# A two-layer S5 / HGRN2 decoder step on one core: HGRN's sample values spread by transfers, a narrower first level, one table product and one memory column moved

## The chip, the cores and the metric

One core of a Trainium2 chip runs the whole kernel; nothing is shared with other cores. The metric is the device time of one launch in microseconds (us), taken as the median of several runs. TensorE is called PE in the profile, VectorE DVE, ScalarE ACT, GpSimd POOL and SyncE SP.

## The reference, cut to what matters

Two layers process 512 prompt tokens and 8 sample rows, each of width 1024. A layer is a half-step SwiGLU FFN, a mixer, cross-attention into 256 memory tokens, and a second half-step FFN. The mixer of layer 0 is S5, that of layer 1 is HGRN2 with 8 heads, each with a 128 x 128 state.

```python
def trunk(x, s5_re, s5_im, hg_s, mem_k, mem_v, lower_bounds, p):
    for i in range(DEPTH):
        x = x + 0.5 * swiglu(rmsnorm(x, ...), p['ffn1_w_in'][i], p['ffn1_w_out'][i])
        h = rmsnorm(x, p['mix_norm'][i])
        if i % N_MIXERS == 0: y, hr, hi = s5_mixer(h, ...)
        else:                 y, sn = hgrn2_mixer(h, hg_s[j], ...)
        x = x + y
        x = x + cross_attend(rmsnorm(x, ...), mem_k[i], mem_v[i], ...)
        x = x + 0.5 * swiglu(...)
# HGRN2, one chunk of 64 tokens of one head:
        att = jnp.einsum('bthk,bshk,btshk->bhts', qc, kc, decay)
        s_new = jnp.exp(btot)[..., None] * s + jnp.einsum('bshk,bshv->bhkv', k_dec, vc)
# for a sample row (one token): S = diag(f) S + k v^T, o = S^T q
# S5: bu from b_bar = (lam_bar - 1) / lam * b, a complex scan over time, y = Re(C h) + d u
# memory: kk, vv = split(rmsnorm(mem, g) @ w_kv)
```

## The kernel before

**Tiles.** Activations are held feature-major, as columns of 520 tokens (512 prompt, 8 sample), split into a front of 256 and a rear of 264. Weights stream from HBM by SP in pieces of 128 output columns ("chunks"). ACT rounds a chunk to w_hi (line 1330), DVE computes the remainder w_lo (line 1827), and PE makes three products for each tile: hi x hi and lo x hi in line 3019, hi x lo in line 3024. A chunk with 1024 input rows is 48 matmuls. The work of the mixers is put between such chunks, on the same in-order PE queue. Small products go to the four PSUM banks called mis, large ones to those called lin.

**The order of small products.** Lists written in the kernel (PREP and K_OUT, S5_ORDER and KV_AFTER, HG; lines 613 to 685) give groups of small products in order. Each group fills one bank, bank number = group number modulo 4, and `reuse` makes PE wait until the group four places earlier was emptied by DVE or ACT. Which chunk a group follows is fixed by the hooks of the lists.

**S5's tables.** While layer 0's first FFN runs, POOL computes for each pair of groups a the tables sFe and sGe (lines 1179 to 1191; each is three operations of lines 736 to 738). PE transposes sFe (groups F, line 2560) and multiplies sGe with bZ (group K, lines 2567 and 2570). Each pair a = 0..3 has its F, F, K behind chunk pair a of the output projection, which has 11 row blocks (66 matmuls a chunk). POOL alternates between two buffers of sGe; for table a it waits for K(a-2).

**Memory columns.** In S5's mixer itself, PE transposes and folds the inputs (X, U, FU, Y groups; line 2732 is U and FU) while ACT and DVE scan. Sixteen column blocks of the memory's keys and values (kv 0 to kv 15, line 2512, three times 8 products each) are spread over it. kv 0, 1 and 2 follow FU 15, the last of the fold groups. The first needs m_hi and m_lo, the normalized memory tokens, which SP reloads from HBM with two transfers of 1 MB (line 818).

**HGRN.** hg_in runs 8 iterations of four chunks (plus two to drain). Between the chunks of head h stand the small products of head h-1 and h-2: S (the sample's output row from the state sS, line 2786), V and K (transposes of values and keys, line 2800), A (attention by level: level 32, 16, 8 in line 2812 from decayed copies lvl, and the diagonal in line 2815), T and N, D (state increments, line 2838), **B** (line 2820: the value column of each of the 8 sample rows, broadcast to 128 columns and transposed, so that a bank holds it on every partition; two groups of four), O (outputs, lines 2853 and 2861) and R (line 2876). DVE updates the prompt state in `states` (lines 2202, 2206) and then the sample states with eight operations (line 2316), sS = value x key + sS, which read B's banks. Then it splits the next weights. SP's queue in an iteration: weights (line 966), prompt state out (908), sample states out (910), the next head's sample states in (921).

## Time and profile before

| | us |
|---|---|
| median of 3 runs (2360.42 to 2362.08) | 2360.5 |
| the profiled execution, whole | 2360.95 |
| its span in the trace | 2359.2 |
| PE busy in the span | 2335.6 (99%) |
| DVE / ACT / POOL busy | 1295.1 / 869.1 / 605.4 |
| mean granted TensorE clock | 0.998 |

PE is busy for all but 24 us of the span. So an edit matters only by what it takes from PE's queue, by the waits of PE that it makes or ends, and by the stretches in which PE is granted less than its full clock; in the clock column 1.00 is 2.4 GHz and 0.50 is 1.2 GHz. A timeline row groups neighbouring instructions of one kind: where it starts, how long it lasts, how many (x), and in brackets how long the engine sat idle before it and what released it. Some products are recorded as two instructions.

### The profile page before, as it was taken

To read this page: it belongs to the slowest core of one execution; us is meant where nothing else is said; L and a number is where in the kernel's file an instruction comes from. 1 tells how busy PE (TensorE), PEld (TensorE's weight loads), DVE (VectorE), ACT (ScalarE), POOL (GpSimd) and SP (SyncE) were. 2 spreads that over 40 slices of the span, in tenths; PEclk is the share of its full clock that TensorE was granted. 3 is DMA by queue.
4 is the path that set the end of the run, shared out by engine and by line. 5 is a ranking of instruction groups with operands and counts; after the bars stand their busy time and mean duration, and the time that the engine had idled before them with its cause. 6 is when DMAs were issued, how large, how long until landed. Compare 5 with 4: busy or idle time off the path is not lost.

```text
span 2359.2 us, 50146 instructions
## 1 busy us (share of the span) xinstructions
PE 2335.6 (99%) x21043; PEld 2273.7 (96%) x21043; DVE 1295.1 (55%) x1906; ACT 869.1 (37%) x1399; POOL 605.4 (26%) x591
## 2 busy tenths in 40 slices
PE   9999999999999999999999999999999999999999
PEld 8999999889979999999999999999999979999999
DVE  6653643964576443445543344577777666443443
ACT  4432333453233321322433233267775233321323
POOL 3779967431103000004111010432122102000003
PEclk9999999999999999999999999999999999999999
DMA  5456445553563333333543333233332653333332
GB/s 160 130 160 153 122 136 165 175 171 107 161 245 86 98 99 89 98 96 98 159 118 111 100 108 115 83 100 107 104 108 77 214 188 91 97 94 94 98 94 94
DMA packets 483707, 289.19 MB, mean 123 GB/s; under 512 B 22289, under 2 KB 466962, under 8 KB 482514
## 3 DMA queue, kind: packets, MB, share of 16 engines
q1 hardware_dynamic: 477856, 280.66, 40.3%
q0 software_dynamic: 560, 1.84, 0.6%
q10 hardware_dynamic: 5122, 4.25, 0.5%
q8 instruction: 129, 2.11, 0.4%
q14 instruction: 40, 0.33, 0.0%
HBM read 258.86 MB, written 27.85 MB: 122 GB/s over the span
## 4 chain that ended last, share of the span: by engine, by line
PE 91%; DVE 4%; POOL 2%; ACT 1%; issue 1%; DMA 1%; SPq 0%; DVEq 0%; POOLq 0%; ACTq 0%
PE lin L3019 51%; PE lin L3024 25%; PE mis L2512 4%; PE mis L2650 1%; PE mis L2633 1%; POOL sTmp L737 1%; PE lin L2600 1%; PE lin L2762 1%; PE lin L2981 1%; PE lin L2757 1%; POOL sGe L738 0%; PE lin L2650 0%; DVE w_lo L1827 0%; PE mis L2626 0%; POOL sFe L738 0%
## 5 line engine op out<-in xcount | busy, mean ns | idle before, releaser
L1827 DVE TENSOR_TENSOR w_lo<-raw,w_hi 128x1024 fp32r<-128x1024 f32 (+1 forms) x322 | 463.8, 1440 | 294.4 <-ACT w_hi L1330 293.7
L1330 ACT ACTIVATE w_hi<-raw 128x1024 fp32r<-128x1024 f32 (+1 forms) x328 | 365.1, 1113 | 311.3 <-PE lin L3024 257.7
L3019 PE MATMUL lin<-a_rear,w_hi 128*128 128x264 f32 x3552 | 455.6, 279 | 0.0
L3019 PE MATMUL lin<-a_front,w_hi 128*128 128x256 f32 x3552 | 451.6, 279 | 1.1 <-DVE a_rear L1840 0.7
L3019 PEld LDWEIGHTS lin<-a_rear,w_hi 128*128 128x128 f32 x3552 | 432.7, 188 | 0.0
L3019 PEld LDWEIGHTS lin<-a_front,w_hi 128*128 128x128 f32 x3552 | 424.5, 188 | 4.6 <-issue 1.8
L3024 PE MATMUL lin<-a_rear,w_lo 128*128 128x264 f32 x1776 | 245.1, 278 | 0.0
L3024 PE MATMUL lin<-a_front,w_lo 128*128 128x256 f32 x1776 | 240.6, 277 | 0.9 <-DVE w_lo L1827 0.9
L2391 DVE SCALAR_TENSOR_TENSOR xT<-lin,xT 128x520 f32<-128x520 f32 (+1 forms) x87 | 60.8, 699 | 322.9 <-PE lin L3024 322.2
L1063 POOL TENSOR_TENSOR acc<-xT 128x520 f32<-128x520 f32 x8 | 12.2, 1520 | 864.0 <-DVE xT L2391 836.0
L3024 PEld LDWEIGHTS lin<-a_rear,w_lo 128*128 128x128 f32 x1776 | 223.8, 188 | 0.0
L3024 PEld LDWEIGHTS lin<-a_front,w_lo 128*128 128x128 f32 x1776 | 219.6, 188 | 1.6 <-DVE w_lo L1827 1.5
L1741 ACT ACTIVATE f_front<-t 128x256 fp32r<-128x256 f32 (+1 forms) x88 | 36.9, 419 | 398.3 <-DVE t L2372 398.3
L3019 PE MATMUL lin<-f_rear,w_hi 128*128 128x264 f32 x1386 | 179.9, 283 | 0.0
L3019 PEld LDWEIGHTS lin<-f_rear,w_hi 128*128 128x128 f32 x1386 | 172.1, 189 | 0.2
L3019 PE MATMUL lin<-f_front,w_hi 128*128 128x256 f32 x1386 | 170.3, 276 | 0.0
L3019 PEld LDWEIGHTS lin<-f_front,w_hi 128*128 128x128 f32 x1386 | 163.3, 188 | 0.0
L1737 ACT ACTIVATE t<-t 128x520 f32<-128x520 f32 x88 | 56.5, 642 | 270.4 <-DVE t L2366 270.4
L2370 DVE TENSOR_TENSOR t<-lin,rstd 128x520 f32<-128x520 f32 x88 | 61.5, 699 | 161.4 <-PE lin L3024 161.4
L1067 POOL TENSOR_TENSOR sqt<-xT 128x520 f32 (+1 forms) x54 | 81.9, 1517 | 211.0 <-DVE xT L2391 148.8
L3019 PE MATMUL lin<-g_all,w_hi 128*128 128x264 f32 (+1 forms) x1024 | 128.8, 278 | 0.0
L3019 PEld LDWEIGHTS lin<-g_all,w_hi 128*128 128x128 f32 x1024 | 122.7, 188 | 1.1 <-DVE g_all L1967 1.1
(512 smaller groups left out, 3182.7 us busy)
## 6 DMA issues: line engine op xcount, KB each, us to landing
raw<-in_ffn_w_in_dram SPq DMA_DIRECT2D x176, 512.0 KB, 3.9
raw<-in_ffn_w_out_dram SPq DMA_DIRECT2D x64, 704.0 KB, 4.6
kc<-in_cache_mem_k_dram SPq DMA_DIRECT2D x32, 512.0 KB, 6.8
vc<-in_cache_mem_v_dram SPq DMA_DIRECT2D x16, 1024.0 KB, 9.7
raw<-in_hg_w_in_dram SPq DMA_DIRECT2D x32, 512.0 KB, 4.2
raw<-in_xattn_w_kv_dram SPq DMA_DIRECT2D x16, 512.0 KB, 4.4
raw<-in_s_w_glu_dram SPq DMA_DIRECT2D x16, 512.0 KB, 3.9
raw<-in_xattn_w_q_dram SPq DMA_DIRECT2D x16, 512.0 KB, 3.9
```

The costliest lines, as they stand in the source:

```text
L737: link(eng.tensor_tensor(tmp, pv[1], mv[1 - e], ALU.mult))
L1067: step.link(pool.tensor_tensor(sqt[:], tile(xT, m), tile(xT, m), ALU.mult))
L1330: act.activation(w_hi[:, j, 0:kt, :], raw[:, j, 0:kt, :], ACT.Copy).then_inc(hi_ready, 1)
L1737: act.activation(t2[:], t1[:], ACT.Silu).then_inc(gate_out, 1)
L1741: ins = act.activation(tile(out, i), t3[:, cols], ACT.Copy)
L1827: dve.tensor_tensor(low_weights(n, j), raw[:, j, 0:kt, :], w_hi[:, j, 0:kt, :].bitcast(F32), ALU.subtract).then_inc(lo_ready, 1)
L2370: step.link(dve.tensor_tensor(t4[:], lflat(1), rstd[:], ALU.mult))
L2391: dve.scalar_tensor_tensor(out=tile(xT, m), in0=lflat(j), scalar=scale, in1=tile(xT, m), op0=ALU.mult, op1=ALU.add)\
L2512: ins = pe.matmul(kv_bank(c)[:, 0:NM], w[:, e, k, :], x[:, k, :], start=k == 0 and u == 0, stop=k == KD - 1 and u == 2)
L2600: ins = pe.matmul(lin[32 * h:32 * h + NS, 1, 0, 0:NM], pZ[:, t, h, b, :], vc[layer][V_SLOT[b]][:, t, h * NM:(h + 1) * NM], start=False, st ...
L3019: pe.matmul(lpart(j, half), high[:, k, :], (x_lo if u else x_hi)[half][:, k, :], start=start and u == 0 and k == 0, stop=False)
L3024: ins = pe.matmul(lpart(j, half), low[:, k, :], x_hi[half][:, k, :], start=False, stop=k == kt - 1)
```

## The change

There are four edits.

1. **Sample values by transfer.** PE's B groups are gone. For each head SP writes the 128 x 8 sample values from hgV to a scratch in HBM (`values_out`, elements of 4 bytes), and later reads them back into vB with a source that repeats the 8 rows of 128 values for each of the 128 partitions (`values_spread`, 512 KB in runs of 512 bytes). DVE's eight sample operations read vB in place of a PSUM bank and count in a new semaphore, `sampled`, on which PE's S group, ACT's next hgF and SP's hg_s transfer wait. For head 0 the sample operations stand behind the split of the next weights; the last head's two transfers stand behind the second load of hg_out's weights. A head has 15 groups instead of 17, so the groups four places earlier change: the O groups wait for N and A's diagonal group, no longer for D; the R groups wait for D.
2. **First level.** The level with 32 tokens (HC is 64) multiplies with the 32 early columns as weights, not with all 64.
3. **Table product.** K(2) moves from behind pair 2 of the output projection to the start of what follows pair 3, ahead of F 6, F 7 and K(3).
4. **Memory column.** kv 0 moves from behind FU 15 to behind FU 11.

```diff
+    vB = [at(f"vB{e}", [P, NS, P], F32, (o_hid + 6 * HTILE, o_tmp + 5 * TILE)[e]) for e in range(2)]
+    hg_v = nc.dram_tensor("hg_v", (HH, NS, P), F32, kind="Internal").ap()
...
         if 0 <= g < HH:
-            made += [("D", (g, 0), "dve"), ("D", (g, 1), "dve"), ("B", (g, 0), "dve"), ("B", (g, 1), "dve")]
+            made += [("D", (g, 0), "dve"), ("D", (g, 1), "dve")]
             made += [("O", (g, 0), "act"), ("O", (g, 1), "act")]
...
+    (late, end), (_, after_late) = PREP["ffn1_out0", 0, 2], PREP["ffn1_out0", 0, 3]
+    PREP["ffn1_out0", 0, 2], PREP["ffn1_out0", 0, 3] = (late, end - 1), (end - 1, after_late)
...
+        if (what, a) == ("FU", 11):
+            S5_ORDER += [("kv", c) for c in KV_AFTER[None][:1]]
         if q + 1 == S5G.after("FU"):
-            S5_ORDER += [("kv", c) for c in KV_AFTER[None]]
+            S5_ORDER += [("kv", c) for c in KV_AFTER[None][1:]]
...
+            def values_out(h):
+                sp.wait_ge(used[0], first_pair["hg_in", 1] + 2 * h + 2)
+                sp.dma_start(hg_v[h].rearrange("b v -> v b"), hgV[h % 2][:, SEQ:NT],
+                             allow_slow_non_contiguous=True).then_inc(spread_out, 16)
+            def values_spread(h):
+                sp.wait_ge(spread_out, 16 * (h + 1))
+                if h >= 2:
+                    sp.wait_ge(sampled, h - 1)
+                    sp.wait_ge(spread_in, 16 * h)
+                src = bass.AP(tensor=hg_v.tensor, offset=h * NS * P, ap=[[0, P], [P, NS], [1, P]])
+                sp.dma_start(vB[h % 2][:], src).then_inc(spread_in, 16)
...
                         if first and j == 1 and ST[n][0] == "hg_out":
+                            values_out(HH - 1)
+                            values_spread(HH - 1)
                             for h in range(HH - 2, HH):
                                 states(h)
...
                             sample_states_in(i // 2)
-                        elif i >= 4:
-                            states(i // 2 - 2)
+                            if i >= 3:
+                                values_spread(i // 2 - 1)
+                        elif i >= 2:
+                            values_out(i // 2 - 1)
+                            if i >= 4:
+                                states(i // 2 - 2)
...
                 def values(p, b):
                     dve.wait_ge(chunk_done, 2 * p + 3)
+                    if p >= p0 + 4:
+                        dve.wait_ge(spread_out, 16 * ((p - p0) // 2 - 1))
...
+                def sample_states(g):
+                    dve.wait_ge(spread_in, 16 * (g + 1))
+                    for f in range(2):
+                        dve.wait_ge(hg["s_decay"], 2 * g + f + 1)
+                        for u in range(4):
+                            s_ = 4 * f + u
+                            ins = dve.scalar_tensor_tensor(
+                                out=sS[g % 2][:, s_], in0=vB[g % 2][:, s_],
...
-                    if 0 <= g < HH:
-                        for f in range(2):
-                            q = G.at("B", (g, f))
...
+                    if 0 < g < HH:
+                        sample_states(g)
                     if 0 < h < HH:
                         split(p + 2, 0, hg_chunk(h, 2))
+                    if g == 0:
+                        sample_states(g)
...
                 if what == "S":
-                    G.emptied_of(pe, "B", (a, 1))
+                    pe.wait_ge(sampled, a + 1)
...
-                            ins = pe.matmul(bank[rows, t * HC // 2:(t + 1) * HC // 2].rearrange("p (b t) -> p b t", t=level),
-                                            lvl[u][:, c], late, start=True, stop=True)
+                            early = level if 2 * level == HC else HC
+                            ins = pe.matmul(bank[rows.start:rows.start + early, t * HC // 2:(t + 1) * HC // 2]
+                                            .rearrange("p (b t) -> p b t", t=level),
+                                            lvl[u][:, c.start:c.start + early], late, start=True, stop=True)
```

PE's queue around the table products of pairs 2 and 3 (L2560 is F, L2567 and L2570 are K; f_front and f_rear are the FFN's hidden activations), first in the kernel before, behind the second chunk of pair 2:

```order
L3024 MATMUL lin<-f_rear_61,w_lo_1_58 128x264 x11
L2560 MATMUL mis<-ident,sTF_235 128x128 x8
L2567 MATMUL mis<-sGe_199,bZ 32x128 x8
L2570 MATMUL mis<-dD,ident 32x16 x4
L3019 MATMUL lin<-f_rear_61,w_hi 128x264 x11
```

and after, at the same place and behind pair 3:

```order
L3054 MATMUL lin<-f_rear_61,w_lo_1_58 128x264 x11
L2595 MATMUL mis<-ident,sTF_237 128x128 x8
L3049 MATMUL lin<-f_rear_61,w_hi 128x264 x11
...
L3054 MATMUL lin<-f_rear_61,w_lo_1_58 128x264 x11
L2602 MATMUL mis<-sGe_201,bZ 32x128 x8
L2605 MATMUL mis<-dD,ident 32x16 x4
L2595 MATMUL mis<-ident,sTF_237 128x128 x8
L2602 MATMUL mis<-sGe_202,bZ 32x128 x8
```

K(2) has passed two chunks and now stands directly ahead of F 6, F 7 and K(3).

PE's queue in S5's mixer at the end of the fold groups (L2732, after the change L2767) and the start of the memory columns (L2512, after the change L2547), before:

```order
L2732 MATMUL lin<-sU,sTF_236 64x80 x24
L2732 MATMUL mis<-sU,sTF_236 64x80 x16
L2732 MATMUL lin<-sU,sTF_236 64x80 x24
L2512 MATMUL mis<-m_hi_103,w_hi 128x256 x8
L2512 MATMUL mis<-m_lo_105,w_hi 128x256 x8
```

and after:

```order
L2767 MATMUL lin<-sU,sTF_238 64x80 x24
L2767 MATMUL mis<-sU,sTF_238 64x80 x8
L2547 MATMUL mis<-m_hi_103,w_hi 128x256 x8
L2547 MATMUL mis<-m_lo_105,w_hi 128x256 x8
L2547 MATMUL mis<-m_hi_103,w_lo_56 128x256 x8
L2767 MATMUL mis<-sU,sTF_238 64x80 x8
L2767 MATMUL lin<-sU,sTF_238 64x80 x24
```

The three times 8 products of kv 0 now split the fold groups: 32 products stand behind them.

SP's queue in one iteration of hg_in, from the second weight pair to the next one, before:

```order
L908 DMA out_hg_p_dram<-hS 128x128 [waits hg_void_dve]
L910 DMA out_hg_s_dram<-sS_177 128x8x128 [waits hg_void_dve]
L966 DMA raw<-in_hg_w_in_dram 128x8x128 [waits lo_ready] x2
L921 DMA sS_177<-in_state_hgrn_dram 128x8x128 [waits hg_fill,hg_s_out]
L966 DMA raw<-in_hg_w_in_dram 128x8x128 [waits lo_ready] x2
```

and after:

```order
L923 DMA hg_v<-hgV_162 128x8x1 [waits used0]
L916 DMA out_hg_p_dram<-hS 128x128 [waits hg_void_dve]
L918 DMA out_hg_s_dram<-sS_177 128x8x128 [waits sampled]
L989 DMA raw<-in_hg_w_in_dram 128x8x128 [waits lo_ready] x2
L944 DMA sS_177<-in_state_hgrn_dram 128x8x128 [waits hg_fill,hg_s_out]
L933 DMA vB_187<-hg_v 128x1024 [waits spread_in,sampled,spread_out]
L989 DMA raw<-in_hg_w_in_dram 128x8x128 [waits lo_ready] x2
```

Two transfers joined the queue: one ahead of the states' outputs, one behind the load of the next sample states.

## Rows read from the trace of the kernel before

**Rows 1.** The page's part 1: busy us, share of span, instructions.

```profile
PE 2335.6 (99%) x21043; PEld 2273.7 (96%) x21043; DVE 1295.1 (55%) x1906; ACT 869.1 (37%) x1399; POOL 605.4 (26%) x591
```

**Rows 2.** Waits of PE: engine line, releaser: us in total, times, longest.

```profile
PE lin L2732 <- issue: 2.1, 1, 2.1
...
PE mis L2853 <- DVE hS L2206: 0.8, 1, 0.8
```

**Rows 3.** Timeline of PE, one head of HGRN (start, us, what).

```profile
1648.60 1.09 PE L2820 MATMUL mis<-ident,hgV 128*128 128x128 f32 x8
1649.45 2.13 PE L3019 MATMUL lin<-a_front,w_hi 128*128 128x256 f32 x16
...
1659.89 1.07 PE L3024 MATMUL lin<-a_front,w_lo 128*128 128x256 f32 x8
...
1665.29 1.59 PE L2812 MATMUL mis<-lvl 128*64 128x32 f32 x48
1666.81 0.44 PE L2792 MATMUL mis<-ident,sRow 128*128 128x128 f32 x2
```

**Rows 4.** Timelines of PE and DVE, head 0 of HGRN.

```profile
1595.67 1.19 PE L3024 MATMUL lin<-a_front,w_lo 128*128 128x256 f32 x8 [0.51 <-DVE w_lo L1827]
...
1591.49 2.15 DVE L2316 SCALAR_TENSOR_TENSOR sS<-mis,hgK,sS 128x128 f32<-128x128 f32 x8
1593.56 2.06 DVE L1827 TENSOR_TENSOR w_lo<-raw,w_hi 128x1024 fp32r<-128x1024 f32 x1
```

**Rows 5.** Timeline of DVE, the next iterations and the last head.

```profile
1650.29 0.69 DVE L2188 TENSOR_TENSOR hgV<-lin,rstd 128x520 f32<-128x520 f32 x1
...
1655.90 1.21 DVE L1827 TENSOR_TENSOR w_lo<-raw,w_hi 128x1024 fp32r<-128x1024 f32 x1
...
1685.88 2.16 DVE L2316 SCALAR_TENSOR_TENSOR sS<-mis,hgK,sS 128x128 f32<-128x128 f32 x8
...
1798.25 2.06 DVE L2316 SCALAR_TENSOR_TENSOR sS<-mis,hgK,sS 128x128 f32<-128x128 f32 x8
```

**Rows 6.** Timeline of SP, and the transfers issued in 1640:1700.

```profile
1664.44 0.37 SPq L921 DMA_DIRECT2D sS<-in_state_hgrn_dram  x1
...
sS<-in_state_hgrn_dram SPq DMA_DIRECT2D x2, 512.0 KB, 4.7
```

**Rows 7.** Timeline of PE at the table products of pairs 2 and 3.

```profile
196.92 0.64 PE L2567 MATMUL mis<-sGe,bZ 128*32 128x128 f32 x16 [2.84 <-POOLq L1191]
197.36 0.26 PE L2570 MATMUL mis<-dD,ident 128*32 128x16 f32 x8
197.54 4.47 PE L3019 MATMUL lin<-f_rear,w_hi 128*128 128x264 f32 x22
...
215.88 0.64 PE L2567 MATMUL mis<-sGe,bZ 128*32 128x128 f32 x16 [0.31 <-ACT sTF L1462]
```

**Rows 8.** Timeline of POOL at the same place.

```profile
193.87 2.86 POOL L738 TENSOR_TENSOR sGe<-sGe,sTmp 128x576 f32<-128x576 f32 x1
...
214.26 1.42 POOL L738 TENSOR_TENSOR sGe<-sGe,sTmp 128x576 f32<-128x576 f32 x1
```

**Rows 9.** Windows: us, busy PE, PEld, DVE, ACT, POOL; PEclk, DMA, GB/s.

```profile
197.30:216.30 19.00, 18.69 (x176) 18.45 (x168) 6.08 (x5) 3.69 (x5) 17.27 (x13) 0.91 0.50 116
```

**Rows 10.** Timelines of PE and DVE at the first memory columns.

```profile
434.69 1.61 PE L2732 MATMUL lin<-sU,sTF 128*64 128x80 f32 x41 [2.05 <-issue]
436.23 1.20 PE L2512 MATMUL mis<-m_hi,w_hi 128*128 128x256 f32 x8
...
438.97 0.29 DVE L2130 COPY sFH<-hs 128x128 f32<-128x128 f32 x1
```

**Rows 11.** Timeline of SP, and the transfers issued in 426:446.

```profile
427.05 0.43 SPq L818 DMA_DIRECT2D m_lo<-mem_split  x1
...
m_lo<-mem_split SPq DMA_DIRECT2D x1, 1024.0 KB, 8.0
```

**Rows 12.** Windows of 1 us, as in rows 9, at the stall.

```profile
433.00:434.00 1.00, 0.00 (x0) 0.00 (x0) 0.96 (x2) 0.00 (x0) 0.00 (x0) 1.00 0.35 131
```

More of the change, by code:

```diff
@@ L453, in trunk_kernel @@
            "scaled_dve", "front", "state_out", "s_decay", "s_out", "squares", "inverse")}
-    rows_in = [sem(f"rows_in{b}") for b in range(NS)]
+    rows_in = [sem(f"rows_in{b}") for b in range(4)]
+    spread_out, spread_in, sampled = sem("spread_out"), sem("spread_in"), sem("sampled")
     consts_done = sem("consts_done")
@@ L2308, in hg_in @@
                         states(g)
-                    if 0 <= g < HH:
-                        for f in range(2):
-                            q = G.at("B", (g, f))
-                            dve.wait_ge(hg["s_decay"], 2 * g + f + 1)
-                            dve.wait_ge(hg["fill"], q + 1)
-                            for u in range(4):
-                                s_ = 4 * f + u
-                                ins = dve.scalar_tensor_tensor(
-                                    out=sS[g % 2][:, s_], in0=hg_bank(q)[:, u * P:(u + 1) * P],
-                                    scalar=hgK[g % 2][:, SEQ + s_:SEQ + s_ + 1], in1=sS[g % 2][:, s_],
-                                    op0=ALU.mult, op1=ALU.add)
-                            ins.then_inc(hg["void_dve"], 1)
+                    if 0 < g < HH:
+                        sample_states(g)
                     if h == HH:
```

14 lines of the change are left out of this document (5 added, 9 removed).

## The prediction, made before the changed kernel was run

> **What bounds the kernel now.** I read the page's busy times first: PE is busy for 2335.6 us of a span of 2359.2 [rows 1]; no other engine comes near. So time can only be won from PE's own instructions, its waits, or stretches at a lower clock. The list of PE's waits comes next: of its entries behind the kernel's start the largest two are at places that the change touches, 2.84 us at the table product (released by POOL) [rows 7] and 2.1 us in the fold groups (released by nothing that the profile shows), and another touched one is 0.8 us at HGRN's outputs [rows 2]. Then I read the timelines of PE, DVE, SP and POOL there. I sum against the profiled execution, 2360.95 us; the median of the runs is 0.45 us lower, and I take that off at the end.
>
> **Edit 1, the sample values.** What leaves PE: the eight transposes start at 1648.60 and the next chunk starts at 1649.45, a slot of 0.85 us [rows 3]. They stand in every one of the 8 heads: 8 x 0.85 = 6.8 us. Nothing waits there for another engine, so the chunks behind move up by that much, if the others follow.
>
> Do they? DVE: the remainder w_lo is split from 1655.90 for 1.21 us, so it ends at 1657.11 [rows 5]; PE takes it at 1659.89 [rows 3], 2.78 us later. With PE 0.85 us earlier 1.9 us are left. The sample multiplies of DVE stay (8 in 2.15 us), with another source. SP: the values are written by DVE from 1650.29 for 0.69 us [rows 5], so they can be sent from 1651.0. The spread is issued behind the load at 1664.44 [rows 6], near 1664.9, and is needed by the multiplies of the next iteration at 1685.88 [rows 5]: 21 us. Its size is that of the load of sS, which landed after 4.7 us [rows 6]. The first transfer is 1024 elements of 4 bytes, which no row shows: from nothing to some 10 us, and 14 us lie between the two issues. I count both at nothing; the cover is the 21 us and the 14 us. On SP's queue the spread puts about 0.4 us (a transfer's issue, as the row at 1664.44) ahead of the next two loads of weights, which wait for DVE's splits and not for SP.
>
> Head 0 is tighter: there PE waits 0.78 us for DVE's states [rows 2], and 0.51 us for w_lo, which DVE makes from 1593.56, behind the multiplies of 2.15 us at 1591.49 [rows 4]. In the new order these multiplies stand behind that split, so the 0.51 us go. The 0.78 us: the O groups now reuse banks that A and N emptied, and only the second half of the outputs, which reads the states, needs them; the 16 products ahead of it cover the wait. So head 0 keeps its 0.85 and gains 0.5. In the last head S waits for the multiplies, which run from 1798.25 for 2.06 us [rows 5]; of that head's 0.85 about 0.25 is turned into a wait. Sum: -6.8 - 0.5 + 0.25 = -7.05 us, with bounds -7.3 (all of it) and -5.8 (head 0's whole and the last head's slot lost).
>
> The Trainium skill has a rule that speaks against this edit (SBUF — State Buffer, "Who interferes with whom"): a DVE instruction with two SBUF inputs contends with a GpSimd instruction that reads SBUF, and the one that starts first keeps the shared ports for its whole length; the multiplies now have two SBUF inputs instead of one. The trace agrees so far as POOL's line 738 takes 2.86 us at one time and 1.42 at another [rows 8]. By that rule the multiplies could be held up by one POOL instruction in each head, which the 1.9 us above would take up; the sum would not change.
>
> **Edit 2, the first level.** Line 2812's 24 products take 1.52 us, from 1665.29 to 1666.81 [rows 3]: 63 ns each. Products with 32 columns as weights are seen elsewhere: eight of line 2567 in 0.44 us (55 ns, 128 moving columns), four of line 2570 in 0.18 us (45 ns, 16 moving columns) [rows 7]. The changed eight have 32 moving columns; at 50 ns they save 8 x 13 = 0.1 us a head. But a tile of another size now stands in front of the second level. I take -0.1 a head, -0.8 in all, since the 1.52 us already hold one such change; bounds are -1.7 (all eight at 37 ns) and +0.8 (the extra change costs 0.2 and nothing is saved).
>
> Edits 1 and 2 together: **-7.9 us**, between -9.0 and -5.0.
>
> **Edit 3, the table product.** It should end the 2.84 us at 196.92 and the slow stretch behind it. Behind the wait PE runs at a lower clock: the window 197.3 to 216.3 has 0.91 of full clock, so 19.0 x 0.09 = 1.7 us are lost in it [rows 9], and its first 22 products take 4.47 us [rows 7]. Both look like a gain of 4.5 us. But behind the next two chunks stands K(3), at 215.88 [rows 7], and its table comes from POOL at 214.26 + 1.42 = 215.68 [rows 8]. POOL was busy for 17.27 of those 19.0 us [rows 9] and has no slack; its work isn't touched. So PE can't pass that place before 215.9, whatever it wins ahead of it. Without the wait and the slow stretch PE comes there 2.84 + 1.7 = 4.5 us earlier and waits 4.5 + 0.3 us there instead of 2.84 once. That is zero, and then the slow clock: before, it followed the wait and lay ahead of POOL's gate, where it cost nothing; now it follows the longer wait and lies behind the gate, where nothing takes it up: +1.7 us. It is paid only if the clock falls again; after 2.84 us of idle it did, so after 4.8 I expect it. DVE's splits also fall earlier relative to POOL's table, and one more POOL operation can be 1.4 us longer (2.86 against 1.42, [rows 8]); I put 0.3 on that. Edit 3: **+2.0**, bounds 0 (no fall of the clock) and +3.1 (1.7 + 1.4).
>
> **Edit 4, the memory column.** It moves work into the 2.05 us stall that ends at 434.69 [rows 10]. But kv 0 needs m_lo, issued at 427.05, which landed 8.0 us after: 435.05 [rows 11], later than the end of the stall. So the stall is not filled. When does PE reach kv 0 behind FU 11? The stall began at 434.69 - 2.05 = 432.64. Behind FU 11 stand 8 products in mis and 24 in lin, 64 records, of which 41 ran behind the stall, in 436.23 - 434.69 = 1.54 us or 0.038 each [rows 10]; the other 23 ran ahead of it in 0.9. So PE is there at 431.75 and waits to 435.05: 3.3 us in place of 2.05, which is +1.3, and the 64 records follow. If the stall itself came from something that is done by 434.7, it is not added. Two more changes of tile size are in the queue, some 0.1 us. DVE has finished its scan at 438.97 [rows 10]; the first output group comes behind kv 2, later at either time, so nothing else is late. The clock stayed at 1.00 in the stall of 2.05 us [rows 12]; it fell behind the one of 2.84. With 3.3 us I expect a fall, and take 1.4 us for it (somewhat under the 1.7 above, since more of what follows is light work). Edit 4: **+2.8**, bounds +0.4 (the transfers land 1 us earlier, no fall) and +3.3.
>
> **The sum.** -7.9 + 2.0 + 2.8 = -3.1 us, so 2357.85 against the profiled 2360.95, and 2357.4 as a median.
>
> **The rivals.**
> - *One gate or both, but no fall of the clock.* PE was at full clock through the 2.05 us stall, which speaks for it; the fall at 198 us speaks against it. Then edit 3 is +0.3, edit 4 is +1.4: -6.2, 2354.3 us.
> - *The moves do what they seem meant for.* Both waits vanish and the clock with them: -7.9 - 2.84 - 1.7 - 2.05 = -14.5, 2346.0 us. For it speaks that the rows of the waits stand just there; against it that POOL's table ends at 215.68 and m_lo lands at 435.05 whatever PE does. It would need POOL to be released by PE somewhere, which its rows don't show.
> - *The transfer is late (slower).* vB is read 128 times from one piece of 4 KB, which no row shows. The mechanism: DVE waits for it in front of the multiplies, and PE behind that for w_lo, in each of 8 heads. It decides when landing takes more than 21 + 1.9 = 23 us, against 4.7 for a plain load of the same size. At 24.5 us it costs 1.5 x 8 = +12: with the rest, 2369.4 us.
> - *The clock falls longer, or the drain between tile sizes costs all of edit 2's bound:* +1.6 and +1.1 on the sum, 2360.1 us, no change.
>
> The Trainium skill says of tile sizes (TensorEngine Tiling (Array Packing), "Key Properties") that changing the mode drains the engine. Edit 2 adds one such change a head and edit 4 two; by that rule edit 2 would lie at its upper bound and the total near 2359, which is within the range.
>
> **How the numbers follow.** My forecast with its bounds has a chance of 0.55, the rival without a fall of the clock 0.20, that with both waits gone 0.08, the late transfer 0.07, the last one 0.10. The predicted time is 2357.4. The range goes from 2352.5 (below the rival without a fall, with edits 1 and 2 at their best) to 2361.0 (above the last rival); outside lie the two rivals of 0.08 and 0.07 and a little of the rest. A measurement of this kernel can tell 0.2%, 4.7 us, from no change: below 2355.8 is faster, above 2365.2 slower. Faster takes the two fast rivals and a sixth of my own case, 0.37; slower the late transfer and a little, 0.08; the same 0.55.
>
> **What would show it.** In the changed profile: the chunk behind D starts where the eight transposes stood, and an iteration of PE is some 0.95 us shorter. Behind pair 3 PE waits some 4.8 us for POOL in front of K(2) or K(3), near 215 us, with windows at 0.50 behind it. In the mixer kv 0 starts near 434 to 435 with a wait of some 3 us before it. vB lands within 10 us, and no engine waits for `spread_in`. I am wrong if PE arrives at K(3) without a wait, if kv 0 starts before 433, or if DVE stands in front of the sample multiplies.

## The result: 0.3% slower, where 0.1% faster was forecast

The changed kernel takes 2367.6 us (median of 8 runs, 2366.1 to 2373.7), the kernel before 2360.5 us in the same comparison (2357.3 to 2363.8). The ratio is 1.0030 with a 95% interval from 1.0021 to 1.0039: 7.1 us slower, where 3.1 us faster was forecast, and outside the range of 2352.5 to 2361.0. The profiled execution took 2366.34 us with a span of 2364.6.

The page of the changed kernel, its part 1, and then its list of PE's waits (engine, line, what released it; us in total, times, longest). They answer to [rows 1] and [rows 2]; lines of the changed kernel are some 30 higher.

```profile
PE 2329.7 (99%) x20979; PEld 2265.8 (96%) x20979; DVE 1304.0 (55%) x1906; ACT 869.3 (37%) x1399; POOL 610.1 (26%) x591
...
PE mis L2602 <- POOLq L1220: 5.1, 1, 5.1
PE mis L2547 <- issue: 3.6, 1, 3.6
PE lin L3054 <- DVE w_lo L1856: 2.8, 7, 0.7
PE lin L2930 <- DVE w_lo L1856: 1.5, 1, 1.5
PE mis L2848 <- ACT vTok L1666: 1.4, 1, 1.4
...
PE mis L2835 <- DVE hO L2269: 1.1, 5, 0.4
PE mis L2821 <- issue: 1.0, 1, 1.0
```

PE is busy for 5.9 us less than before (2329.7 against 2335.6); the slots of the transposes were 6.8, and some of that is taken back by products at half clock. But the span is 5.4 us longer, so PE idles 11 us more. The list says where: the one wait for POOL grew from 2.84 to 5.1 us; the wait at the memory columns is 3.6 us instead of 2.1; and HGRN, which had 0.8 us at `states` and 0.24 and 0.51 at w_lo, now has five of the seven waits for w_lo (2.2 of the 2.8 us), one of 1.5 at the first products of hg_out (line 2930), one for vTok, five for hO.

**The table product.** PE's timeline behind pair 3, answering to [rows 7], and windows of 1 us each (us, busy PE, PEld, DVE, ACT, POOL, then the granted clock, DMA share, GB/s):

```profile
206.97 0.65 PE L2602 MATMUL mis<-sGe,bZ 128*32 128x128 f32 x16
...
213.76 1.08 PE L2602 MATMUL mis<-sGe,bZ 128*32 128x128 f32 x16 [5.08 <-POOLq L1220]
...
214.85 2.93 PE L3049 MATMUL lin<-a_front,w_hi 128*128 128x256 f32 x12
217.58 2.68 PE L3049 MATMUL lin<-a_rear,w_hi 128*128 128x264 f32 x12
...
212.17 1.40 POOL L746 TENSOR_TENSOR sGe<-sGe,sTmp 128x576 f32<-128x576 f32 x1
...
214.00:215.00 1.00, 1.00 (x25) 0.96 (x17) 0.00 (x0) 0.02 (x1) 0.78 (x1) 0.50 0.92 258
...
217.00:218.00 1.00, 1.00 (x6) 1.00 (x6) 1.00 (x1) 0.00 (x0) 0.92 (x2) 0.50 0.17 35
```

K(2) runs at once, K(3) waits for POOL, whose table ends at 212.17 + 1.40 = 213.57. (This trace runs some 2.2 us ahead of that of before from the first table product on.) Behind the wait the clock is at half for some 6 us, and the first 12 products of the chunk take 2.73 us, from 214.85 to 217.58.

**The memory column.** PE's timeline there, answering to [rows 10], SP's issue, the landing, and two windows:

```profile
434.67 1.79 PE L2547 MATMUL mis<-m_hi,w_hi 128*128 128x256 f32 x8 [3.63 <-issue]
436.25 1.91 PE L2547 MATMUL mis<-m_lo,w_hi 128*128 128x256 f32 x8
437.96 1.28 PE L2547 MATMUL mis<-m_hi,w_lo 128*128 128x256 f32 x8
439.17 0.77 PE L2767 MATMUL mis<-sU,sTF 128*64 128x80 f32 x16
...
426.27 0.43 SPq L826 DMA_DIRECT2D m_lo<-mem_split  x1
...
m_lo<-mem_split SPq DMA_DIRECT2D x1, 1024.0 KB, 8.3
...
433.00:434.00 1.00, 0.00 (x0) 0.00 (x0) 1.00 (x1) 0.00 (x0) 0.00 (x0) 1.00 0.04 16
...
436.00:437.00 1.00, 1.00 (x7) 1.00 (x6) 0.97 (x2) 0.00 (x0) 0.00 (x0) 0.50 0.00 0
```

m_lo lands at 426.27 + 8.3 = 434.6, kv 0 starts at 434.67, and then PE is at half clock until some 438.3. The profile ends this wait with "issue", which only says that it saw no engine behind it; the time of landing tells what it was.

**HGRN.** Where the gain should have come. One iteration in the middle (PE's and DVE's timelines), to be held against [rows 3] and [rows 5]:

```profile
1654.33 1.16 PE L2870 MATMUL mis<-vTok,kTok 64*128 64x128 f32 x16
1655.42 2.10 PE L3049 MATMUL lin<-a_front,w_hi 128*128 128x256 f32 x16
...
1670.94 0.66 PE L2835 MATMUL mis<-ident,outK 128*128 128x128 f32 x4 [0.16 <-DVE hO L2269]
1671.53 1.50 PE L2848 MATMUL mis<-lvl 128*32 128x32 f32 x48
1672.96 0.44 PE L2827 MATMUL mis<-ident,sRow 128*128 128x128 f32 x2
...
1685.71 1.16 PE L2870 MATMUL mis<-vTok,kTok 64*128 64x128 f32 x16
...
1660.70 3.48 DVE L2249 SCALAR_TENSOR_TENSOR sS<-vB,hgK,sS 128x128 f32<-128x128 f32 x8
1664.11 1.21 DVE L1856 TENSOR_TENSOR w_lo<-raw,w_hi 128x1024 fp32r<-128x1024 f32 x1
...
1659.88 1.30 POOL L1325 TENSOR_TENSOR outK<-outK,hgK 128x512 f32<-128x512 f32 x1
1661.13 1.32 POOL L1327 TENSOR_TENSOR inQ<-inQ,hgQ 128x512 f32<-128x512 f32 x1
```

The slot of the transposes is gone (the chunk follows at 1655.42, 1.09 us behind the increments). An iteration takes 1685.71 - 1654.33 = 31.38 us. But DVE's eight sample operations take 3.48 us instead of 2.16 [rows 5], while POOL scales outK and inQ, and PE waits for hO (0.16) behind them. And this is a good iteration. The starts of the increments of heads 0, 1, 2, 3 lie at 1586.86, 1620.69, 1654.33 and 1685.71: the first two steps are 33.83 and 33.64 us, where the kernel before has 32.99 and 32.05.

### The profile page after: what moved, and what is told of

Read it like the earlier page. It is cut to its first block, busy times and chain, and to the rows that moved or that the text cites. A ratio compares the mean times of both kernels' runs of the same rounds, so it can differ in the third digit from the quotient of the medians.

```text
span 2364.6 us, 50038 instructions
## 1 busy us (share of the span) xinstructions
PE 2329.7 (99%) x20979; PEld 2265.8 (96%) x20979; DVE 1304.0 (55%) x1906; ACT 869.3 (37%) x1399; POOL 610.1 (26%) x591
## 4 chain that ended last, share of the span: by engine, by line
PE 83%; DVE 6%; ACT 4%; POOL 3%; issue 2%; DMA 2%; SPq 0%; DVEq 0%; ACTq 0%; POOLq 0%
PE lin L3049 47%; PE lin L3054 23%; PE mis L2547 4%; POOL sTmp L745 1%; DVE sS L2249 1%; DMA raw<-in_hg_w_in_dram 1%; PE mis L2685 1%; PE mis L2668 1%; DVE w_lo L1856 1%; ACT w_hi L1359 1%; POOL sGe L746 1%; PE lin L2797 1%; DVE hS L2237 1%; POOL sFe L746 1%; PE lin L2792 1%
```

## The experiments

Each kernel is timed together with the kernel before on one chip; the comparison runs give that kernel 2360.1 to 2361.1 us. The ratio in the tables is not the quotient of the two medians. Four theories stand against each other. **G**: edits 3 and 4 only move PE's waits for POOL and for m_lo, and the clock falls behind them. **S**: with two operands in SBUF the sample operations share reads with POOL, and DVE hands on late. **T**: the transfer of 1024 elements of 4 bytes holds up what is queued behind it. And the prediction's own sum for edit 1.

### Each edit alone

```diff
 # e1_kv_only: the kernel before, and
+        if (what, a) == ("FU", 11):
+            S5_ORDER += [("kv", c) for c in KV_AFTER[None][:1]]
         if q + 1 == S5G.after("FU"):
-            S5_ORDER += [("kv", c) for c in KV_AFTER[None]]
+            S5_ORDER += [("kv", c) for c in KV_AFTER[None][1:]]
 # e2_table_only: the kernel before, and
+    (late, end), (_, after_late) = PREP["ffn1_out0", 0, 2], PREP["ffn1_out0", 0, 3]
+    PREP["ffn1_out0", 0, 2], PREP["ffn1_out0", 0, 3] = (late, end - 1), (end - 1, after_late)
```

e3_level_only adds edit 2 to the kernel before; e4_values_only is the changed kernel without edits 2, 3 and 4.

> The kernel before with edit 4 alone (kv 0 behind FU 11). Theory G (the transfer of m_lo is the gate): kv 0 waits more than 3 us for it, starts near 434.7 to 435, and the clock falls behind the wait: +2.8 to +3.5 us against the kernel before, so about 2363.5. Rival (the move fills the stall): -2 us, 2358.5. Rival (gate, but no fall of the clock): +1.3, 2361.8.

> The kernel before with edit 3 alone (K(2) behind pair 3). Theory G (POOL's table 3 is the gate, the slow clock is paid behind it): one wait of 4.5 to 5.1 us in place of 2.84, then some microseconds at half the clock: +1.7 to +3, about 2362.5 to 2363.5. Rival (the wait goes): -2.8 to -4.5, 2356 to 2357.7. Rival (gate without the clock): 0, 2360.5.

> The kernel before with edit 2 alone (32 weight columns in the first level). Theory: the level products take 1.43 instead of 1.52 us in each of 8 heads: -0.7 us, 2359.8, within noise of no change. Rival (the extra change of tile size drains PE): +0.8, 2361.3.

> The kernel before with edit 1 alone (sample values by transfer). Theory P (losses outweigh: sample multiplies of 3.2 to 4.0 us instead of 2.15, and weights that land late behind the 4-byte transfer in the first and the last head): +2 to +3 against the kernel before, about 2363, with the multiplies long in every head that POOL works beside, and ACT waiting some 6 us for a weight transfer near 1575. Rival (the prediction's own sum: the transposes go and the rest is hidden): -7, about 2353.5, if the losses in the changed kernel came only from its being shifted against other engines by edits 3 and 4.

| kernel | median us | before us | ratio (95%) |
|---|---|---|---|
| edit 4 alone | 2363.6 | 2360.4 | 1.0020 (1.0009 to 1.0032) |
| edit 3 alone | 2363.6 | 2360.4 | 1.0011 (1.0002 to 1.0020) |
| edit 2 alone | 2360.5 | 2360.4 | 0.9998 (0.9989 to 1.0007) |
| edit 1 alone | 2362.6 | 2360.4 | 1.0006 (0.9997 to 1.0015) |

The differences of the medians are +3.2, +3.1, +0.1 and +2.2, together 8.6 against the 7.1 of the whole change: it adds up to within what these medians can tell. By the ratios edit 4 costs from 2.1 to 7.6 us: four of its eleven executions lie at 2367.9 to 2371.2 us, with a mean clock of 0.995 or 0.996, the other seven at 2360.6 to 2363.6. Theory G holds for both moves. In the trace of edit 3 alone K(3) waits 5.08 us, as in the changed kernel:

```profile
213.94 1.08 PE L2569 MATMUL mis<-sGe,bZ 128*32 128x128 f32 x16 [5.08 <-POOLq L1193]
...
217.00:218.00 1.00, 1.00 (x7) 1.00 (x7) 1.00 (x1) 0.00 (x0) 0.92 (x2) 0.50 0.32 55
```

From the second table product to the first group of S5's mixer this edit costs 3.0 us in both traces that have it (229.86 us before, 232.92 and 232.85 with it). That a slow clock ahead of POOL's gate costs nothing can be seen in the trace of e14 below, which has the old order: K(2) waits its 2.85 us there, the clock stays full behind it, and K(3) then waits 2.14 us for POOL. The same stretch is 229.92 us long. Edit 2 is nothing that can be measured; in the changed kernel's rows above the level products take 1.43 us (1671.53 to 1672.96) instead of the 1.52 of [rows 3]. (The profiled execution of edit 2 alone is the slowest of its eleven, 2365.11 us.) Edit 1, from which 7 us were to come, costs time by itself.

### Taking the two suspected causes of edit 1 away

```diff
 # e5_long_runs: edit 1 alone, and
-    vB = [at(f"vB{e}", [P, NS, P], F32, ...
-    hg_v = nc.dram_tensor("hg_v", (HH, NS, P), F32, kind="Internal").ap()
+    vB = [at(f"vB{e}", [P, P, NS], F32, ...
+    hg_v = nc.dram_tensor("hg_v", (HH, P, NS), F32, kind="Internal").ap()
...
+                sp.dma_start(hg_v[h], hgV[h % 2][:, SEQ:NT]).then_inc(spread_out, 16)
...
+                                out=sS[g % 2][:, s_], in0=vB[g % 2][:, :, s_],
 # e6_behind_split: edit 1 alone, and
-                    if 0 < g < HH:
-                        sample_states(g)
...
-                    if g == 0:
+                    if 0 <= g < HH:
                         sample_states(g)       # behind split(p + 2, 0, ...) for every head
 # e7_pool_short: edit 1 alone, and
-                    pool.tensor_tensor(outK[:], outK[:], hgK[e][:, 0:SEQ], ALU.mult)
+                    pool.tensor_tensor(outK[:, 0:8], outK[:, 0:8], hgK[e][:, 0:8], ALU.mult)
 # (and the same for inQ)
 # e13_short_out: edit 1 alone, and
-                sp.dma_start(hg_v[h].rearrange("b v -> v b"), hgV[h % 2][:, SEQ:NT], ...
+                sp.dma_start(hg_v[h], hgV[h % 2][0:NS, 0:P])
```

e8_both is e5 and e6; e14_both_away is e13 and e7. Three of these kernels leave something out: e7 and e14 two parts of the decay, and e13 and e14 send 4 KB of other values, from 8 partitions instead of 128.

> Edit 1 alone, but the scratch holds the 8 sample values of a partition side by side: the first transfer is 128 runs of 32 bytes instead of 1024 of 4, the spread reads runs of 4 KB instead of 512 bytes, and DVE reads vB with a stride of 8 elements. Theory T (the small runs delay the weights of the first head and the spread of the last): the 6.3 us idle of ACT before its weights near 1575 and the 10.5 us wait of SP for the first transfer go, and the time falls by 2 to 3 us against edit 1 alone (2362.6), to about 2360. Rival (only the shared reads of DVE and POOL matter): no change from edit 1 alone, 2362.6.

> Edit 1 alone, with the sample multiplies behind the split of the next weights in every head, not only in head 0. Theory S (shared reads: the multiplies are slow where POOL works beside them and delay w_lo): the multiplies fall back to about 2.1 us, because POOL is done by then, but the split may be the one that POOL holds up (1.2 to some 2.4 us, as in head 0); PE's waits for w_lo of 0.66, 0.71 and 1.49 us go, 2360 to 2361. Rival (the multiplies are slow by their operands alone): still 3.2 us and more, and the time stays at 2362.6.

> Edit 1 alone, with POOL's two scalings that run beside the multiplies (outK x hgK and inQ x hgQ, 512 columns each) cut to 8 columns; this leaves out that part of the keys' and queries' decay, so its output differs. Theory S (shared reads): DVE's eight multiplies take 2.15 us again in every head and PE's waits for w_lo and hO go: 1.5 to 3 us faster than edit 1 alone, about 2360. Rival (slow by their operands): 3.2 us and more, 2362.6.

> e5 and e6 together: long runs and the multiplies behind the split. If both causes are real and independent, the gains add: 2362.6 - 2.5 - 2 = about 2358, and the slot of the transposes begins to show as a gain. If one of them hides the other: 2360. Rival of the prediction's sum (all of 7 us): 2353.5.

> Edit 1 alone, but the first transfer sends 8 runs of 512 bytes from other data in hgV (the sample values it sends are wrong, so the sample states differ); all else, the contiguous reads of vB too, stays. It parts what e5 mixed. Theory T (the 1024 runs of 4 bytes hold up the weights of the first heads and the last spread): ACT's idle of 6 us near 1575 and PE's waits for vTok and w_hi go, head 0's increments start some 1.2 us sooner, and the time is 1.5 to 3 us under edit 1 alone, 2359.5 to 2361. Rival (the small runs are harmless): 2362.6.

> e13 with POOL's two scalings cut to 8 columns as in e7 (two parts of the computation left out). If shared reads and small runs are the whole account, the prediction's sum for edit 1 comes back: -6 to -7 us against the kernel before, about 2354, iterations of 31.1 us from the first. If the time stays at e7's 2358.9, something third holds the first heads back.

| kernel | median us | before us | ratio (95%) |
|---|---|---|---|
| edit 1 alone (above) | 2362.6 | 2360.4 | 1.0006 (0.9997 to 1.0015) |
| e5 long runs, strided reads | 2364.4 | 2361.1 | 1.0015 (1.0006 to 1.0024) |
| e6 multiplies behind the split | 2365.5 | 2361.1 | 1.0020 (1.0011 to 1.0029) |
| e8 e5 and e6 | 2371.0 | 2361.1 | 1.0046 (1.0032 to 1.0060) |
| e7 POOL's two scalings cut | 2358.9 | 2361.1 | 0.9995 (0.9986 to 1.0004) |
| e13 first transfer in 8 runs | 2359.9 | 2360.1 | 0.9997 (0.9988 to 1.0006) |
| e14 e13 and e7 | 2353.4 | 2360.1 | 0.9970 (0.9960 to 0.9981) |

**S** is shown by e7. DVE's timeline in e7, the same place in edit 1 alone, and then DVE and POOL in the kernel before:

```profile
1652.28 2.18 DVE L2245 SCALAR_TENSOR_TENSOR sS<-vB,hgK,sS 128x128 f32<-128x128 f32 x8
...
1656.38 3.47 DVE L2245 SCALAR_TENSOR_TENSOR sS<-vB,hgK,sS 128x128 f32<-128x128 f32 x8
...
1653.83 2.15 DVE L2316 SCALAR_TENSOR_TENSOR sS<-mis,hgK,sS 128x128 f32<-128x128 f32 x8
...
1653.00 1.30 POOL L1296 TENSOR_TENSOR outK<-outK,hgK 128x512 f32<-128x512 f32 x1
1654.25 1.29 POOL L1298 TENSOR_TENSOR inQ<-inQ,hgQ 128x512 f32<-128x512 f32 x1
```

Without POOL's two scalings the eight operations take 2.18 us, with them 3.47; the operand in SBUF costs nothing by itself. Nor does POOL by itself: in the kernel before, the eight operations ran beside the same two scalings, with their values in PSUM, and took 2.15 us. It takes both, which is what the rule that the prediction names says; what the two engines share there no run shows by itself. Three of the six full iterations of e7 are 31.09 us, those of edit 1 alone 31.4, those of the kernel before 32.05. So with nothing in the way edit 1 gives 0.96 us a head. PE's rows in e14 say from what: the slot of 0.84 us, and 0.12 us by which the chunk behind it is shorter when no transposes stand in front of it (5.73 against 5.85 us).

e6 is a miss that teaches something: behind the split the operations do fall to 2.18 us in most heads, but PE's next V and K groups wait for DVE's addition to hO (0.27 to 1.59 us, four times), and the S group of the last head but one waits 2.8 us. The delay was moved to another hand-over of DVE, not taken away. The profiled execution of e6 is its slowest (2372.1 us), and in it the clock is at half for some 6 us behind the wait of 1.59 us and for more than 8 us behind that of 2.8. e8, for which 2358 us was expected, missed by 13: its strided operations still take 3.0 us behind the split in most heads, PE waits 1.0 to 1.2 us for hO in each of four middle heads, and 3.6 us at S.

**T** is shown by e13. ACT's timeline near the first head, first in edit 1 alone, then in e13 (w_hi is the split of a weight chunk, raw its transfer), with the median landing times of the weights issued in 1560:1582:

```profile
1574.26 1.06 ACT L1355 ACTIVATE w_hi<-raw 128x1024 fp32r<-128x1024 f32 x1 [5.68 <-DMA raw<-in_hg_w_in_dram]
1575.22 0.58 ACT L1662 ACTIVATE vTok<-mis 128x512 f32<-128x512 f32 x1
...
raw<-in_hg_w_in_dram SPq DMA_DIRECT2D x3, 512.0 KB, 8.3
...
1569.00 1.05 ACT L1354 ACTIVATE w_hi<-raw 128x1024 fp32r<-128x1024 f32 x1
1569.95 0.58 ACT L1661 ACTIVATE vTok<-mis 128x512 f32<-128x512 f32 x1
...
raw<-in_hg_w_in_dram SPq DMA_DIRECT2D x3, 512.0 KB, 5.4
```

With 1024 runs of 4 bytes ahead of them the weights land after 8.3 us instead of 5.4, ACT sits idle for 5.68 us, and vTok, which stands behind that split on ACT, is made at 1575.22 instead of 1569.95: PE waits 0.67 us for it. (In the changed kernel it is 9.0 us, 6.31 us idle, and PE waits 1.4 us.) From the first chunk of hg_in to the increments of head 3 edit 1 alone takes 2.5 us more than e13 (139.56 against 137.06). The wait of SP for the same transfer in the last head of the changed kernel is the row below; there the spread can't be issued before.

```profile
SPq L933 <- DMA hg_v<-hgV: 10.5, 1, 10.5
```

The Trainium skill (DMA: Bandwidth & Descriptors, "Rules for kernel authors") says that a transfer whose last dimension is not contiguous becomes one descriptor for each element. The profiles agree. Queue q1 (packets, MB, share), in edit 1 alone and in e13:

```profile
q1 hardware_dynamic: 487328, 284.89, 41.7%
...
q1 hardware_dynamic: 479136, 284.89, 41.0%
```

The bytes are equal, and there are 8192 packets more, 1024 for each of the eight transfers. e13 sends 4 KB in 8 runs and has neither the late weights nor the wait of SP. But the wait of SP in the last head costs PE nothing. The spread was in time in all eight heads: no engine waits for it, and DVE starts the last head's sample operations 5.06 us behind the last increments with the wait (1803.64 against 1798.58 in the changed kernel) and without it (e13). T is paid at the first heads only.

e5 could not show T, though its first head has no wait for vTok either: its layout made DVE's reads strided, and the eight operations took 4.0 to 4.1 us in the middle heads and 2.81 in the last, where POOL is idle (2.09 with contiguous reads). One number hid the other, which is why e13 was made.

**Both together are the whole.** e14 is 6.7 us under the kernel before; the prediction's sum for edit 1 was 7.05. Its increments start 31.27 us apart in the first step and 31.09 in each one up to the drain. So nothing third of a size that could be seen is left. Each median taken against the kernel before of its own comparison, e7 is 4.3 us better than edit 1 alone, e13 2.4, and e14 8.9, more than the 6.7 of the two: where one cause is left, it takes up part of what the other gives back. S costs 4.3 us beside T and 6.5 without it, T 2.4 beside S and 4.5 without it. One control was not run, the kernel before with POOL's two scalings cut. In its middle heads the timeline shows no wait of PE, so the cut could give it nothing there; in the first step, where e14 is 1.72 us shorter than the kernel before, it isn't shown how much of that is the cut.

### Building the change without the two causes

```diff
 # e9_act_pool: edits 1 and 2, DVE's sample operations taken off it
+                        for s_ in range(NS):       # ACT, behind its split
+                            ins = act.activation(vB[g % 2][:, s_], vB[g % 2][:, s_], ACT.Copy,
+                                                 scale=hgK[g % 2][:, SEQ + s_:SEQ + s_ + 1])
...
+                    for u in range(0, NS, 2):      # POOL, behind inQ
+                        ins = pool.tensor_tensor(sS[g % 2][:, u:u + 2], sS[g % 2][:, u:u + 2], vB[g % 2][:, u:u + 2], ALU.add)
 # e16_rows: e9, and the values sent as rows (in the last head DVE does the sample operations)
+                    if u == 0:                     # PE, in the first level's group
+                        ins = pe.transpose(bank[0:NS, P:2 * P], hgV[h % 2][:, SEQ:NT], ident[:])
...
+                        dve.tensor_copy(vrow[:], hg_bank(q)[0:NS, P:2 * P])
...
+                HG.emptied_of(sp, "A", (h, 0))
+                sp.dma_start(hg_v[h], vrow[:]).then_inc(spread_out, 16)
 # e11_products_later: the kernel before, K(2) as in edit 3 and K(3) behind the next pair
+    PREP["ffn1_out0", 0, 2], PREP["ffn1_out0", 0, 3] = (late, end - 1), (end - 1, after_late - 1)
+    PREP["ffn1_in1", 0, 0] = (after_late - 1, after_late)
```

e10_act_pool_long is e9 with e5's layout, e12_combined is e9 and e11, e17_rows_later is e16 and e11.

> Edits 1 and 2 without 3 and 4, and DVE's eight sample operations are taken off DVE: ACT multiplies vB by the key column in place (behind its w_hi split, where it idled), POOL adds the product to sS in four pieces behind its own scalings. Theory S (DVE, slowed by the reads that it shares with POOL, is what gives the gain back): an iteration of PE falls to 31.0 to 31.1 us, no wait for w_lo or hO behind the third head, and about 5 us are won from the kernel before, 2355.5, the first two heads and the last keeping some loss. Rival (the transfers themselves, not DVE, hold the gain back): no better than edit 1 alone, 2362. Rival (POOL's additions meet DVE's splits and S waits for them): 2360 to 2363 with PE waiting at S.

> e9 with the scratch laid out as in e5 (first transfer 128 runs of 32 bytes, spread in 4 KB runs, ACT and POOL read with a stride). Theory T (the transfer of 4-byte runs holds up the weights behind it in the first heads, 1.15 us there, and the last head's spread by 10 us): 1 to 1.5 us faster than e9, if the strided reads cost ACT and POOL nothing that shows; rival (the stride costs more, as it did DVE in e5): equal or slower than e9.

> The kernel before, with K(2) where edit 3 puts it and K(3) moved on too, to behind the first chunk pair of the next stream. Theory G (POOL's tables gate, one every 19 us, and edit 3 alone only moves the wait): neither product waits now, PE gets through 4.5 us earlier until K(4), which POOL's fifth table ends near 236.4, so PE waits up to 2 us there: -2.5 to -4 us, about 2357.5. Rival (the waits are made up for elsewhere, or the clock falls behind the wait at K(4)): 0, 2360.5.

> e9 and e11 together. They are 1300 us apart, so the gains should add: if e9 gives 5 and e11 3 us, 2352.5, 0.3% below the kernel before; if both theories fail, 2360 or more.

> e9 with the values sent as rows: PE transposes the 8 sample columns once into a free part of the first level's bank, DVE copies the 8 x 128 block, SP sends 8 runs of 512 bytes and spreads them from between the next two weight loads; in the last head DVE does the sample operations. All outputs are computed. Theory S plus T: the gain of e14 without leaving work out, 2354 to 2356. Rival (ACT, POOL or SP's queue is late by the longer chain from the first level to the spread): PE waits at S or for w_lo, 2358 to 2362.

> e16 and e11 together: both gains add if they hold, 2352 to 2354, 0.3% under the kernel before and 0.6% under the changed kernel. If e16 fails: 2358 or more.

| kernel | median us | before us | ratio (95%) |
|---|---|---|---|
| e9 ACT and POOL | 2364.7 | 2360.6 | 1.0014 (1.0005 to 1.0023) |
| e10 e9, strided | 2372.9 | 2360.6 | 1.0050 (1.0036 to 1.0064) |
| e11 K(2), K(3) later | 2359.1 | 2360.6 | 0.9992 (0.9983 to 1.0001) |
| e12 e9 and e11 | 2361.6 | 2360.6 | 1.0003 (0.9994 to 1.0012) |
| e16 rows, ACT and POOL | 2356.9 | 2360.1 | 0.9986 (0.9977 to 0.9995) |
| e17 e16 and e11 | 2355.1 | 2360.1 | 0.9979 (0.9970 to 0.9988) |

e9 missed by 9 us. Its middle iterations are as expected, 30.86 to 31.33 us, so taking the work off DVE answers S. But it keeps the small runs, and its first heads and its last lose more than that: 1.76 us for vTok, 1.44 for w_lo, 0.91, 1.88 and 2.04 us at S, where PE now waits for POOL. With strided reads (e10) PE waits for POOL's additions in every head, 0.5 to 3.6 us; it was expected a little faster than e9 and came out 8 us slower. e16, which sends 8 runs of 512 bytes, has no wait for vTok and is 3.2 us faster than the kernel before, short of e14's 6.7 and of the 2354 to 2356 us expected: two waits for POOL's additions remain. The rows are those of PE's waits in e16's HGRN:

```profile
1598.26 0.64 PE L2829 MATMUL mis<-sS,hgQ 128*32 128x128 f32 x16 [0.93 <-POOL sS L1317]
...
1784.10 0.64 PE L2829 MATMUL mis<-sS,hgQ 128*32 128x128 f32 x16 [1.78 <-POOL sS L1317]
```

e11 answers the question on the table products. K(2) and K(3) wait for nothing there, and the next product, K(4), waits for POOL instead, at the time at which POOL's next table is ready:

```profile
207.63 0.65 PE L2570 MATMUL mis<-sGe,bZ 128*32 128x128 f32 x16
...
220.60 0.64 PE L2570 MATMUL mis<-sGe,bZ 128*32 128x128 f32 x16
...
235.53 0.65 PE L2570 MATMUL mis<-sGe,bZ 128*32 128x128 f32 x16 [2.10 <-POOLq L1194]
```

From the second table product to S5's mixer it takes 226.96 us, 2.9 less than before. In the three other traces with this order it takes 228.74 (e12), 227.48 (e17) and 228.58 (e18): behind the wait at K(4), of 2.1 to 2.5 us, the clock was at half for some 3.4 us in e12 and e18, and full in e11 and e17. By medians e11 is 1.5 us faster than the kernel before, which its interval just fails to tell from nothing; on top of e9 and of e16 the same edit gives 3.0 and 1.8. e12 and e17 were expected at 2352.5 and at 2352 to 2354 us, and missed, e12 by what e9 had missed.

### The wait for the memory

```diff
 # e15_kv_half_wait: edit 4 alone, and
-                    pe.wait_ge(mem_in[l], 32)
+                    pe.wait_ge(mem_in[l], 48 if l else 16)
...
-                    sp.dma_start(t[l][:].bitcast(F32), mem_split[l, u]).then_inc(mem_in[l], 16)
+                    sp.dma_start(t[l][:].bitcast(F32), mem_split[l, u]).then_inc(mem_in[max(l, u)], 16)
...
+                if l == 0 and c == 0:
+                    terms = [terms[0], terms[2], terms[1]]   # the 8 products with m_lo last, behind their own wait
```

e18_all is e17 with this and edit 4.

> Edit 4 alone, but kv 0 waits only for m_hi (issued first, lands 4.7 us after its issue) ahead of its 16 products with m_hi, and for m_lo (8.4 us) ahead of the last 8. Theory G (edit 4's loss is the wait for m_lo and the slow clock behind it): the 3.7 us wait splits into nothing or little ahead of kv 0 and some 1.5 us ahead of its last products, the clock stays full, and the loss of 3.2 us goes: 2359 to 2360.5. Rival (a stall of PE's instruction issue stands at this place whatever waits; it was 2.05 us in the kernel before): the 2.05 us stay somewhere in these products beside the wait, and the time is 2361 to 2363.

> e17 (rows sent, ACT and POOL form the sample states, K(2) and K(3) later) with e15's form of edit 4. If e15 gains against the kernel before, the same on top of 2355.1: 2353.5 to 2355; if the wait and its clock come back, 2357.

| kernel | median us | before us | ratio (95%) |
|---|---|---|---|
| edit 4 alone (above) | 2363.6 | 2360.4 | 1.0020 (1.0009 to 1.0032) |
| e15 waits by halves | 2359.4 | 2360.7 | 0.9996 (0.9987 to 1.0005) |
| e18 all | 2354.8 | 2360.7 | 0.9970 (0.9960 to 0.9980) |

PE's timeline in e15:

```profile
429.60 1.21 PE L2519 MATMUL mis<-m_hi,w_hi 128*128 128x256 f32 x8
430.64 1.11 PE L2519 MATMUL mis<-m_hi,w_lo 128*128 128x256 f32 x8
432.99 1.22 PE L2519 MATMUL mis<-m_lo,w_hi 128*128 128x256 f32 x8 [1.24 <-DMA m_lo<-mem_split]
434.14 0.77 PE L2739 MATMUL mis<-sU,sTF 128*64 128x80 f32 x16
434.74 1.83 PE L2739 MATMUL lin<-sU,sTF 128*64 128x80 f32 x48
```

The 16 products with m_hi start without a wait, the 8 with m_lo wait 1.24 us, now named as what it is, and the stall of 2.05 us that the kernel before has in its fold groups [rows 10] doesn't come back: the 48 records behind 434.74 run in one piece. The loss of 3.2 us is gone. That settles edit 4 for theory G. What the 2.05 us stall was stays open. In the sixteen traces that have the old order it lasts from 1.50 to 2.33 us, it starts 5.6 to 6.3 us behind the issue of m_lo, and it ends between 0.6 us ahead of that transfer's landing and 0.25 us behind it. So it goes with the transfer, and some of it may be hidden in e15's wait of 1.24 us; no run here moved the transfers.

e18 is the fastest kernel of this case that leaves nothing out, 5.9 us under the kernel before by medians and some 13 us under the changed kernel; its 0.3 us on e17 can't be told from nothing.

## Why the prediction was wrong, step by step

- **What bounds the kernel**: right. Every microsecond lost is a wait of PE or a stretch at half clock.
- **Edit 3, +2.0**: right in its mechanism. It measured +3.1. The term that was too small is the clock: PE was at half for some 6 us behind the wait of 5.1 us (about 3 us lost), where 1.7 us were taken over from the stretch behind the shorter wait. The longer POOL operation, priced at 0.3, did not come (1.40 us).
- **Edit 4, +2.8**: right, +3.2 measured. The wait (3.63 against 3.3 us), its cause (kv 0 starts 0.1 us behind the landing of m_lo) and the fall of the clock behind it were as worked out. That kv 0 starts just at 434.67 is in part luck: this trace ran 2.2 us ahead, lost 3.0 by edit 3, and lacks a slow stretch near 417 in which the kernel before lost 1.7 us. The first rival, that the clock would not fall, is refuted for edit 3 and for edit 4 in two traces each.
- **Edit 2, -0.8**: -0.09 us a head at its products, as worked out; by medians it can't be told from nothing, and neither can the change of tile size that stood against it.
- **Edit 1, -7.05**: this step failed, by 9 us. Its gain is real: e14 measured 6.7 with both causes away. That this is so near 7.05 is partly luck, since the parts were other ones: 0.96 us in a middle head instead of 0.85, 1.72 in the first step instead of 1.35, and 0.09 in the drain instead of 0.6. Two sentences of the step were wrong. "I count both at nothing", on the two transfers: the first one, 4 KB in 1024 runs, was judged by whether it would itself be in time, not by what it does to the weights behind it on the same queues. Its landing was bounded at 10 us, which is about what it took (SP waits 10.5 us); the cover of 14 us was beside the point. It costs 2.4 us. And "the 1.9 us above would take up" the shared reads: the rule was looked up, and its size guessed right (one POOL instruction, 1.3 us of 3.48), but the slack was read for one hand-over only, w_lo in a middle head. DVE also hands hO to PE, and in the first heads and in the drain there is no such slack for w_lo either. It costs 4.3 us.
- **The slower rival** named a transfer that lands too late for the multiplies. The spread was in time in all eight heads (it landed after 4.2 to 8.4 us), though in the last it was issued 10.9 us behind the first transfer. The real slower case was two smaller mechanisms at once, each of which the text mentions and prices at nothing.

## What to carry to other kernels

- Work taken off the busiest engine comes back if what replaces it uses the engine that feeds it. Read the slack at every hand-over of that engine, and in the first and the last round of a loop apart, before a longer operation is called covered.
- A transfer of many tiny runs is to be judged by what is queued behind it. 4 KB in 8 runs instead of 1024 was worth 2.4 us here (e13).
- A wait for one gate costs nothing while a later gate, set by another engine, holds PE anyway; turned into a longer wait at that later gate it cost the clock behind it here, in each of two traces. Before a product is moved to where its input "must be ready", ask what the next gate is: moving two products was a gain where moving one was a loss.

## What the runs showed of the hardware that was not expected

- Eight operations of DVE with both operands in SBUF took 2.18 us beside an idle POOL and 3.47 beside its two multiplications; with one of the two in PSUM they took 2.15 beside the same multiplications. With both in SBUF they took 4.0 to 4.1 when one was read at a stride of 8 elements, and 2.81 with that stride and an idle POOL.
- How long PE had been idle did not by itself tell whether the clock fell behind it. Behind the wait of 2.84 to 2.85 us at K(2) it was at half for some 3.4 us in eleven traces and full in a twelfth (e14). Behind 3.63 and 3.73 us it fell for some 3.4 us, behind 5.08 (two traces) for some 6. Behind 2.05 us in S5's mixer it stayed full in seven traces and fell in an eighth (e3); behind 3.33 us it stayed full in e10, and behind 1.43 us it fell in e5. A prediction can give such a fall a chance, not a certainty.
- Kernels with nothing changed in S5's mixer differ there by up to 5.5 us from one profiled execution to the next: 119.98 us in e2, whose clock is full there, and 125.53 in e3, which loses some 5 us of that in stretches at half clock near 417 and 437. They reach the first table product up to 4.8 us apart. Single traces can't be compared by their spans here; stretches between two landmarks and medians can.
